# The rotary half swap of a two-layer hybrid decoder: VectorE shuffle or TensorE permutation matmul

## The reference, cut to what matters

```python
ROT_DIM = DIFF_HEAD_DIM // 4          # 16; half = 8
def partial_rotary(x, pos):
    ...
    x1 = x[..., :half].astype(jnp.float32)
    x2 = x[..., half:ROT_DIM].astype(jnp.float32)
    rot = jnp.concatenate([x1 * cos - x2 * sin, x2 * cos + x1 * sin], axis=-1)
    return jnp.concatenate([rot.astype(x.dtype), x[..., ROT_DIM:]], axis=-1)

q = partial_rotary(q.reshape(B_, S, 2 * DIFF_HEADS, DIFF_HEAD_DIM), pos)
k = partial_rotary(k.reshape(B_, S, 2 * DIFF_HEADS, DIFF_HEAD_DIM), pos)
```

## Time and profile before

| what | value |
|---|---|
| median of 3 runs | 1266.51 us (1266.21 to 1266.82) |
| profiled execution, its own time | 1266.82 us |
| its span, first to last instruction | 1265.0 us |
| TensorE busy | 1253.0 us (99%), 6129 matmuls |
| weight loads busy | 1019.9 us (81%) |
| VectorE busy | 677.0 us (54%) |
| ScalarE busy | 496.4 us (39%) |
| DMA, mean | 92 GB/s |

### The profile page before, as it was taken

One profiled execution on the slowest core, in us unless ns is written; L12 is line 12 of the kernel. 1 busy time (PEld: TensorE's weight loads), 2 busy tenths in 40 slices (PEclk: granted clock), 3 DMA queues, 4 the chain that ended last, 5 costly groups with the idle time before them and its releaser, 6 DMA issues.

```text
span 1265.0 us, 16409 instructions
## 1 busy us (share of the span) xinstructions
PE 1253.0 (99%) x6129; PEld 1019.9 (81%) x6129; DVE 677.0 (54%) x987; ACT 496.4 (39%) x816; POOL 9.9 (1%) x17
## 2 busy tenths in 40 slices
PE   9999999999999999999999999999999999999997
PEld 7876657888888888888888888888888888888886
DVE  6787877544444442227777667546664444443224
ACT  6344366433333322215584253454343333332223
POOL 0000000000000000000000000000000000000000
PEclk9999999999999999999999999999999999999999
DMA  6332402222222222221222101011243333333221
GB/s 246 106 110 75 126 24 83 97 88 98 99 99 99 99 99 100 99 99 67 101 93 72 45 25 51 34 51 67 83 147 108 101 110 112 104 99 109 91 100 67
DMA packets 50867, 116.61 MB, mean 92 GB/s; under 512 B 21250, under 2 KB 21506, under 8 KB 50818
## 3 DMA queue, kind: packets, MB, share of 16 engines
q1 hardware_dynamic: 49906, 114.58, 27.5%
q10 hardware_dynamic: 912, 1.35, 0.4%
HBM read 107.36 MB, written 2.10 MB: 87 GB/s over the span
## 4 chain that ended last, share of the span: by engine, by line
PE 92%; DVE 4%; ACT 2%; issue 1%; ACTq 0%; DMA 0%; SPq 0%; DVEq 0%
PE PS L1500 91%; PE PS L1576 1%; DVE cacc L1181 0%; ACTq L738 0%; DVE resid L1475 0%; DVE outT L1491 0%; DVE wring L1036 0%; DMA raw<-w_stream 0%; ACT unread L935 0%; DVE amax L1099 0%; PE PS L1799 0%; ACT L859 0%; DVE wbuf L1110 0%; DVE hbuf L1307 0%; ACT pbuf L697 0%
## 5 line engine op out<-in xcount | busy, mean ns | idle before, releaser
L1500 PE MATMUL PS<-HH,wring 128*128 128x512 f32 x3096 | 724.7, 392 | 0.0
L1500 PEld LDWEIGHTS PS<-HH,wring 128*128 128x128 f32 x3096 | 575.1, 188 | 117.1
L1500 PE MATMUL PS<-AA,wring 128*128 128x512 f32 (+1 forms) x792 | 183.0, 390 | 0.4 <-DVE AA L1115 0.3
L1500 PEld LDWEIGHTS PS<-AA,wring 128*128 128x128 f32 x792 | 148.3, 188 | 32.3 <-issue 1.0
L1007 DVE TENSOR_TENSOR ubuf<-PS,rstd 128x512 f32<-128x512 f32 x44 | 30.4, 691 | 192.0 <-PE PS L1500 192.0
L1029 DVE TENSOR_TENSOR wring<-raw,wring 128x1024 fp32r<-128x1024 f32 x36 | 44.1, 1226 | 147.4 <-ACT wring L669 147.4
L1500 PE MATMUL PS<-wring,AA 128*128 128x512 f32 x528 | 119.8, 389 | 0.0
L1500 PEld LDWEIGHTS PS<-wring,AA 128*128 128x128 f32 x528 | 99.1, 188 | 20.6
L1016 DVE TENSOR_TENSOR wring<-raw,wring 128x1024 fp32r<-128x1024 f32 x88 | 107.5, 1222 | 3.5 <-ACT wring L656 3.0
L651 ACT ACTIVATE AA<-ubuf 128x512 f32 x44 | 27.8, 633 | 192.8 <-DVE ubuf L1014 192.8
L1036 DVE TENSOR_TENSOR wring<-raw,wring 128x1024 fp32r<-128x1024 f32 x69 | 84.3, 1225 | 33.6 <-ACT wring L613 33.4
(11 more groups left out here) (274 smaller groups left out, 1032.4 us busy)
## 6 DMA issues: line engine op xcount, KB each, us to landing
raw<-w_stream SPq DMA_DIRECT2D x193, 512.0 KB, 3.2
reps<-ub SPq DMA_DIRECT2D x32, 66.5 KB, 2.1
resid<-turned SPq DMA_DIRECT2D x16, 128.0 KB, 4.8
out_t<-outT SPq DMA_DIRECT2D x3, 512.0 KB, 2.6
reps_b<-ub SPq DMA_DIRECT2D x16, 66.5 KB, 2.1
reps<-ub ACTq DMA_DIRECT2D x16, 66.5 KB, 2.8
xT<-x_t SPq DMA_DIRECT2D x4, 256.0 KB, 5.4
raw<-w_stream SPq DMA_DIRECT2D x4, 256.0 KB, 5.7
```

What stands on the lines that cost most here:

```text
L1500: return nc.tensor.matmul(out, lhsT, rhs, start=start, stop=stop)
```

## The change

The swap of the partition halves is no longer a VectorE shuffle but a TensorE matmul with a 128x128 permutation matrix, which is appended to the rope table (the DMA and the SBUF tile grow from 1024 to 1152 columns; the tiles behind it move up by 512 bytes per partition). TensorE gets the step `("rope", j)`: it waits for the table and for the evacuation of tile j, then multiplies the permutation by `hbuf[:, j % 2]` into the bank that the tile itself had used, both plain float32, 128x128 by 128x512. VectorE now waits for this matmul before its first multiply, and its sine multiply reads the permuted values from PSUM. `bank_free` waits for that sine multiply instead of the evacuation.

```diff
     for p in range(P):
         q = p % 64
         if q < half:
-            rc[p], rs[p] = cos[q], -sin[q]
+            rc[p], rs[p], perm[p + half, p] = cos[q], -sin[q], 1.0
         elif q < 2 * half:
-            rc[p], rs[p] = cos[q - half], sin[q - half]
-    rope = np.concatenate([rc, rs], axis=1).astype(np.float32)
+            rc[p], rs[p], perm[p - half, p] = cos[q - half], sin[q - half], 1.0
+    rope = np.concatenate([rc, rs, perm], axis=1).astype(np.float32)
...
-    rope, q = at("rope", [2 * S], f32, q)
+    rope, q = at("rope", [2 * S + P], f32, q)
...
         def rope_finish(j):
             dve.wait_ge(rope_loaded, 16)
-            dve.wait_ge(evacuated, QK_TILE[j] + 1)
+            dve.wait_ge(sem("rope_mm"), j + 1)
             dst = qk[:, j // 2 + 4 * (j % 2)]
             V.tensor_tensor(dst, hbuf[:, j % 2], rope[:, 0:S], ALU.mult)
-            link(V.stream_shuffle(sqb[:, j % 2], hbuf[:, j % 2], HALF_SWAP))
-            link(V.tensor_tensor(sqb[:, j % 2], sqb[:, j % 2], rope[:, S:2 * S], ALU.mult))
+            V.tensor_tensor(sqb[:, j % 2], PS[:, QK_BANK[j]], rope[:, S:2 * S], ALU.mult).then_inc(sem("rope_sin"), 1)
+            dve.wait_ge(sem("rope_sin"), j + 1)
             V.tensor_tensor(dst, dst, sqb[:, j % 2], ALU.add).then_inc(sem("qk_ready"), 1)
...
             elif before[0] == "q":
-                pe.wait_ge(evacuated, slot_tile(n - 2) + 1)
+                pe.wait_ge(sem("rope_sin"), before[1] + 1)
...
+            elif kind == "rope":
+                pe.wait_ge(rope_loaded, 16)
+                pe.wait_ge(evacuated, QK_TILE[a] + 1)
+                mm(PS[:, QK_BANK[a]], rope[:, 2 * S:], hbuf[:, a % 2]).then_inc(sem("rope_mm"), 1)
```

More of the change, by code:

```diff
@@ L235, in odd_order @@
     return order
-HALF_SWAP = [lane + 8 if lane < 8 else lane - 8 if lane < 16 else lane for lane in range(32)]
 LAMBDA_INIT = 0.8 - 0.6 * math.exp(-0.3 * 0)
@@ L258, in shape_constants @@
     cos, sin = np.cos(ang).astype(np.float32).T, np.sin(ang).astype(np.float32).T
-    rc, rs = np.ones((P, S)), np.zeros((P, S))
+    rc, rs, perm = np.ones((P, S)), np.zeros((P, S)), np.zeros((P, P))
     for p in range(P):
```

## The result

The changed kernel takes 1273.48 us (median of 5 runs, 1273.21 to 1273.75), the kernel before beside it 1266.54 us (5 runs, 1266.21 to 1267.16). The ratio is 1.0058, with a 95% interval of 1.0046 to 1.0069: 6.9 us slower. The forecast was 1273.6. Of seven more executions of the changed kernel four took 1273.17 to 1273.73 us and three 1275.42 to 1275.66, and the kernel before has some that are 2 us longer too; in the profiled execution of experiment 4, which is such a one, 1.8 us of it lie in the head, in front of everything that the change touches.

A forecast was written before the change was run, and what follows sets the result against it. TensorE, busy 99% of the span, was taken as the bound: 7.0 us for eight float32 matmuls plus 0.1 for a late evacuation, on a median of 1266.51, gave 1273.6 us; range 1272.6 to 1276.0.

The forecast's parts named there:

- TensorE's pace is the time: Whole span: TensorE is busy 99%, so a microsecond added to its list should lengthen the run by one.
- The price of the matmul: Eight float32 rope matmuls on TensorE at 0.88 us each, between 0.85 and 0.90: 7.0 us.
- Rival A: Semaphore waits keep rope matmul weights from loading ahead: 0.96 us each plus gaps, 1274.3 to 1275.1 us; chance 0.18.
- The estimate from the Trainium skill's figures: Rope matmuls: four float32 passes at 0.2157 us give 0.863 us each, 6.9 us in all.
- Late evacuations (the 0.1 us): TensorE's rope steps: evacuation of tile 4 late by 0 to 0.29 us, taken as 0.1; the other tiles in time.
- a margin of 0.18: Rope step of tile 3: evacuation ends at 68.67 and TensorE arrives at 68.85, so in time by 0.18 us.
- VectorE's position: Each rope step leaves VectorE later by about 0.6 us at most, TensorE by 0.88, so VectorE's wait costs nothing.
- nothing is given back later: Behind the last rope step: all engines are moved by the same amount, so none of the 7.1 us returns.
- the range's low end: 1272.6 us: 6.8 us of matmuls, no wait, less 0.7 for run spread and part of the wait at 158 us.
- rival C: From 60 to 137 us VectorE sets TensorE's pace, so removed shuffles count: at best 1262 to 1264 us; chance 0.02.
- Bank and table: Later bank release by the sine multiply, and an eighth more bytes in the rope table's DMA: both cost nothing.
- rival B: VectorE's wait makes TensorE wait 0.3 to 0.6 us at six later steps: 1275.7 to 1277.5 us; chance 0.14.

The follow-up runs named there:

- experiment 4: Changed kernel with the permutation matmul in fp32r, one pass instead of four, queries and keys rounded for it: 1268.35 us, ratio 1.0013.
- experiment 1: Kernel before with the eight permutation matmuls added on TensorE; VectorE keeps its shuffles and doesn't wait for the matmuls before its multiplies: 1272.92 us, ratio 1.0046.
- experiment 2: Changed kernel with each permutation matmul made twice in a row: 1280.60 us.
- experiment 6: Changed kernel with the permutation matmul over one column only, the swap left out for all tokens but one, all waits kept: 1268.28 us.
- Experiment 7: Changed kernel with VectorE's cosine multiply done before its wait for the permutation matmul: 1272.99 us.
- experiment 9: Kernel before with each shuffle made twice, nothing added to TensorE: 1268.21 us, ratio 1.0013.

## Why the prediction was right

**TensorE's pace is the time.** Right. +7.06 us at 154.89 are +6.92 at the end. That the median came within 0.1 us of the forecast is in part luck: the runs of one kernel spread by 0.5, the 0.1 us of lateness that the sum holds was less, and 0.1 that it doesn't hold was given back.

**The price of the matmul.** Foreseen 0.88, between 0.85 with hidden loads and 0.90 from four shorter ones; measured 0.86 in the stream with a `diff_v` behind it, 0.90 as a shift with products behind it, and 1.71 for two. The 0.90 of the four shorter matmuls was worked back from 92.12; the start of the products as it is listed, 90.65, would have given 0.81, under the lower bound of 0.85. Rival A, exposed loads, was true at one step of eight, behind the convolution (102.17, its load not ahead). There it cost nothing extra: the `diff_v` behind it had paid for its own exposed load before, and now had it loaded under the rope matmul. Without the correction for the head, the shift grew from 4.10 (89.84 to 93.94) to 5.07 at the `diff_v` behind that rope matmul (98.06 to 103.13) and was back at 4.96 with the next scores (102.56 to 107.52): 0.86 in all. Experiments 1, 2 and 4 show that the loss is the matmuls' own time on TensorE and no wait; experiment 4, with one pass at 0.23 us, and experiment 6, where two loads cost 0.24 at most, leave the passes as the price at 512 columns. The four passes of float32 that the Trainium skill names ("FP8 and Floating Point Precision", TensorE Precision Notes) are borne out: 0.86 us against 0.23 for one. The estimate from the Trainium skill's figures, 6.9 us, is the measured difference; the staircase of the two traces has 7.06 and 0.14 given back, and 0.1 of the 7.06 may be scatter.

**Late evacuations (the 0.1 us).** Half right. At tile 4, where I had the risk, TensorE was in time: the evacuation of the changed kernel ends at 91.92 + 0.68 = 92.60, and the load starts at 92.85. VectorE's lead did carry over 20 us: the evacuation starts 2.51 later (89.41 to 91.92) and TensorE comes 3.24 later, 0.73 more of a lead, where I had worked out 0.75. At tile 3, where I had a margin of 0.18, it was late by 0.05: the weight load is idle for 0.19 in front of the rope matmul and the step costs 3.60 - 2.70 = 0.90; at tile 4 it is 0.86 (the scores in front of it are moved by 3.24, 86.26 to 89.50, the `diff_v` behind it by 4.10). Timeline of weight loads, changed kernel:

```profile
70.21 0.30 PEld L1499 LDWEIGHTS PS<-hbuf,rope 128*128 128x128 f32 x2 [0.19 <-issue]
```

I had measured the margin to the start of the matmul. Elsewhere in the stream its weights start 0.22 us ahead of it, and here they started only 0.07 ahead. Experiment 7 tries this margin: the matmul is the same, and VectorE ends the evacuation earlier. Timelines of weight loads and of TensorE in that kernel:

```profile
69.90 0.41 PEld L1500 LDWEIGHTS PS<-hbuf,rope 128*128 128x128 f32 x2
...
70.13 1.02 PE L1500 MATMUL PS<-hbuf,rope 128*128 128x512 f32 x2
```

There the load is 0.23 ahead, with no idle time in front, and the step costs 0.87 instead of 0.90 (62.60 to 64.74 and 67.97 to 70.98, foot 28.96). So the lateness at tile 3 is real and costs 0.03 to 0.05 us.

**VectorE's position.** The step that failed is "nothing is given back later: behind the last rope step all engines are moved by the same amount"; its size is 0.11 us. VectorE comes out of a rope step 0.59 later, I had worked out, and TensorE 0.88. Timeline of VectorE, changed kernel, against the earlier trace rows:

```profile
63.78 0.69 DVE L1089 TENSOR_TENSOR qk<-hbuf,rope 128x512 f32<-128x512 f32 x1 [1.54 <-PE PS L1499]
64.39 0.68 DVE L1090 TENSOR_TENSOR sqb<-PS,rope 128x512 f32<-128x512 f32 x1
...
65.72 0.54 DVE L1177 TENSOR_SCALAR cacc<-ub,vec 128x512 f32<-128x512 f32 x1
```

The step ends at 65.72 instead of 63.67, +2.05, of which 1.41 were there before (the scores in front of it went from 57.67 to 59.08): 0.64, near the 0.59. The lead that remains reached the `WT` wait as 0.1 us, within the 0.7 by which the range's low end allowed for it. How large it can get was the surprise: 0.65 without any shuffle, and as much with the shuffle and a matmul that VectorE doesn't wait for (experiment 1). The chance that VectorE's removed work would count, rival C, was rightly small: the whole of it was worth 0.65 us. The idle time in front of the cosine multiply, foreseen at about 1 us, was 1.5. More work on VectorE counts for more than less work does: the doubled shuffles cost 1.4 us (experiment 9).

**Bank and table.** As foreseen: the sine multiply from PSUM takes 0.68 us, and no wait for a bank or for the table is listed.

**Sums of the rivals.** Two ends don't add up as they stand, and neither bears on the forecast: six steps at 0.3 to 0.6 us are 1.8 to 3.6 and not 2 to 4, so rival B is 1275.4 to 1277.2, and the upper end of rival A is 1266.5 + 7.7 + 0.8 = 1275.0.

## What to carry to other kernels

When one engine is busy all the time, work that is moved onto it is paid in full, and the work that is freed elsewhere is worth only what a wait in the chain was hanging on: here 7 us paid for at most 0.65. Here a plain float32 matmul of 512 columns cost two instructions of 0.43 us, against 0.23 for one in fp32r, and a small one didn't get cheaper than two weight loads, 0.22. Measure the margin of a matmul that waits for its input to its weight load, not to its own start.

## What the runs showed of the hardware that I had not expected

- A float32 matmul with a 128x128 stationary operand cost nearly the same for 1 column as for 128: +1.90 us at the scores near 154.9 for eight of them with one column (29.54 to 156.81 us in that kernel against 29.52 to 154.89), 0.24 each; with 128 columns it was +2.06 (28.80 to 156.23), 0.26 each, and the medians are +1.6 and +1.9 us. Loads of such weights followed one another at 0.11 us.
- The matmul that had to wait for its data got its weights late too: at 70.21 the load began 0.07 us in front of its matmul, elsewhere in the stream 0.22, and 0.23 in experiment 7, where the data were there earlier.
- Eight DMA issues hold ScalarE's queue for 5.3 us, 0.66 each.
